# Queue order of weight splits, four-head norms and constants in the root, in a 256-token two-block kernel

## Time and profile before

| what | value |
|---|---|
| median of 3 runs | 3174.78 us (3172.57 to 3176.36) |
| the profiled execution | 3182.96 us, its span 3181.1 us |
| TensorE busy | 2980.7 us (94%) |
| VectorE busy | 1983.2 us (62%) |
| ScalarE busy | 1421.4 us (45%) |
| GpSimd busy | 214.3 us (7%) |
| mean granted TensorE clock | 0.965 of full speed |

### The profile page before, as it was taken

The page is one execution under the profiler, slowest core; times in us unless marked ns, Lnnn a source line. Parts: engine busy times, 40 slices in busy tenths (PEclk is TensorE's granted clock), DMA queues, the critical chain, the costliest instruction groups (busy, mean ns, idle before and its releaser), DMA issues.

```text
span 3181.1 us, 55567 instructions
## 1 busy us (share of the span) xinstructions
PE 2980.7 (94%) x23544; PEld 2902.4 (91%) x23544; DVE 1983.2 (62%) x2232; ACT 1421.4 (45%) x1804; POOL 214.3 (7%) x172
## 2 busy tenths in 40 slices
PE   7998889999999999999997999988799999999986
PEld 7988879999999999999997999976699999999986
DVE  5466776655667666666767676755556555555665
ACT  4345544444444444444445444443444444444443
POOL 1010001100000000000001020111100000000010
PEclk9999899999999999999999999987899999999998
DMA  6634443345555665565554633310266556556553
GB/s 195 182 118 133 121 133 112 122 123 167 176 181 174 186 183 175 174 188 173 182 182 129 190 101 120 107 54 1 70 188 185 179 179 192 182 178 191 174 159 107
DMA packets 251817, 482.24 MB, mean 152 GB/s; under 512 B 16784, under 2 KB 22032, under 8 KB 251440
## 3 DMA queue, kind: packets, MB, share of 16 engines
q1 hardware_dynamic: 251568, 478.68, 49.4%
HBM read 476.53 MB, written 2.10 MB: 150 GB/s over the span
## 4 chain that ended last, share of the span: by engine, by line
PE 58%; DVE 21%; ACT 10%; DMA 5%; issue 4%; POOL 1%; DVEq 0%; POOLq 0%; ACTq 0%
PE psm L393 52%; DVE slo L315 8%; PE psb L447 6%; ACT ar L472 4%; ACT shi L313 4%; DVE ar L475 3%; DVE ar L483 3%; DMA raw<-in_w_up 1%; DMA raw<-in_w_down 1%; DMA raw<-in_w_out 1%; DVE x L475 1%; DVE ar L486 1%; DMA raw<-in_w_ple_gate 1%; DVE hf L486 1%; ACT gh L472 1%
## 5 line engine op out<-in xcount | busy, mean ns | idle before, releaser
L315 DVE TENSOR_TENSOR slo<-raw,shi 128x1024 fp32r<-128x1024 f32 (+1 forms) x901 | 1139.7, 1276 | 788.2 <-ACT shi L313 782.5
L313 ACT ACTIVATE shi<-raw 128x1024 fp32r<-128x1024 f32 (+1 forms) x901 | 930.5, 1050 | 942.9 <-PE psm L393 465.6
L393 PE MATMUL psm<-gh,shi 128*128 128x256 f32 x3664 | 1066.5, 291 | 92.5 <-DVE slo L315 75.1
L393 PE MATMUL psm<-gl,shi 128*128 128x256 f32 x3664 | 1047.4, 286 | 0.0
L393 PE MATMUL psm<-gh,slo 128*128 128x256 f32 x3664 | 1047.0, 286 | 0.0
L393 PE MATMUL psm<-hh,shi 128*128 128x256 f32 x3408 | 980.9, 288 | 39.1 <-DVE slo L315 23.8
L393 PE MATMUL psm<-hl,shi 128*128 128x256 f32 x3408 | 972.5, 285 | 0.0
L393 PE MATMUL psm<-hh,slo 128*128 128x256 f32 x3408 | 972.1, 285 | 0.0
L393 PEld LDWEIGHTS psm<-gh,shi 128*128 128x128 f32 x3664 | 712.9, 195 | 105.3 <-DVE slo L315 81.9
L393 PEld LDWEIGHTS psm<-gl,shi 128*128 128x128 f32 x3664 | 713.1, 195 | 3.4 <-issue 2.7
L393 PEld LDWEIGHTS psm<-gh,slo 128*128 128x128 f32 x3664 | 712.4, 194 | 0.3
(11 more groups left out here) (187 smaller groups left out, 1323.0 us busy)
## 6 DMA issues: line engine op xcount, KB each, us to landing
raw<-in_w_in SPq DMA_DIRECT2D x240, 512.0 KB, 3.7
raw<-in_w_up SPq DMA_DIRECT2D x176, 512.0 KB, 4.1
raw<-in_w_ffn_up SPq DMA_DIRECT2D x128, 512.0 KB, 3.9
raw<-in_w_ffn_down SPq DMA_DIRECT2D x128, 512.0 KB, 4.0
raw<-in_w_down SPq DMA_DIRECT2D x88, 512.0 KB, 4.5
raw<-in_w_out SPq DMA_DIRECT2D x64, 512.0 KB, 4.3
raw<-in_w_ple_gate SPq DMA_DIRECT2D x32, 512.0 KB, 4.9
raw<-in_w_branch_b SPq DMA_DIRECT2D x16, 512.0 KB, 4.6
```

The source lines that it names most:

```text
L313: th = A.do(lambda e: e.activation(shi[:, s, 0:m], raw[:, q, 0:m], ACT.Copy), landed, pe_tok.get(j - NS), chain=False, cost=0.22 + 0.82e-3 ...
L315: lo_tok[j] = V.do(lambda e: e.tensor_tensor(slo[:, s, 0:m], raw[:, q, 0:m], shi[:, s, 0:m].bitcast(F), ALU.subtract), landed, th, chain=F ...
L393: e.matmul(out, l, r, start=st, stop=sp, skip_group_check=True),
```

## The change

In the order of one pass for tile j, both parts of a split now stand at the end of the pass: hi of tile j+4 ahead of the epilogue, lo of tile j+4 (with its fetch of tile j+7) behind the epilogue and ahead of the `fgs` step and the background steps. Four tiles instead of three are split before the first pass. `qk_norm` is replaced by `heads_norm(g)`, in lane 2, queued as soon as the convolution of group g (four heads of q or k) is through: the column sums of four heads go with a 32-column matrix of ones to the four 32-partition quarters of one bank, one root and one reciprocal of 128x256 serve all four, and a matmul from 32 rows with `hsel` spreads each head's row over the partitions again. The end of `gdn` does the same for two heads. The roots read PSUM with scale and bias and the separate multiply-adds go.

```diff
+        def split_hi(j):
+            ...
+            hi_tok[j] = A.do(lambda e: e.activation(shi[:, s, 0:m], raw[:, q, 0:m], ACT.Copy),
+                             landed, pe_tok.get(j - NS), chain=False, cost=0.22 + 0.82e-3 * m)
+        def split_lo(j):
+            ...
             lo_tok[j] = V.do(lambda e: e.tensor_tensor(slo[:, s, 0:m], raw[:, q, 0:m],
                                                        shi[:, s, 0:m].bitcast(F), ALU.subtract),
-                             landed, th, chain=False, cost=0.16 + 1.04e-3 * m)
+                             landed, hi_tok[j], chain=False, cost=0.16 + 1.04e-3 * m)
             if j + NR < len(tiles):
                 issue(j + NR)
@@ group
-                if j + NS - 1 < len(tiles):
-                    split(j + NS - 1)
...
                 cur[1] += 1
+                split_hi(j + NS)
                 if ti == len(ts) - 1:
                     slot.free = epi(slot.ap, pe_tok[j])
+                split_lo(j + NS)
                 for _ in range(fg):
                     fg_step()
                 bg_ready()
@@ Norm.finish
-                tv = ts(rb, b.ap[:, 0:256], 1.0 / D, 1e-6, ALU.mult, ALU.add, tp)
-                ta = act(rb, rb, ACT.Sqrt, tv)
+                ta = act(rb, b.ap[:, 0:256], ACT.Sqrt, tp, scale=1.0 / D, bias=C("eps", 0, 1))
...
-                    stt(r2, b.ap[:, 256:512], 1.0 / D, r2, ALU.mult, ALU.mult)
-                    tv = ts(r2, r2, 1e-6, None, ALU.add, None)
-                    ta = act(r2, r2, ACT.Sqrt, tv)
+                    tv = stt(r2, b.ap[:, 256:512], 1.0 / D, r2, ALU.mult, ALU.mult)
+                    ta = act(r2, r2, ACT.Sqrt, tv, bias=C("eps", 0, 1))
@@ before the first group
-            if f < NS - 1:
-                split(f)
+            split_hi(f)
+            split_lo(f)
@@ end of rope
-                bgs[w] += [moba(w), qk_norm(w)]
+                bgs[w].append(moba(w))
@@ in place of qk_norm
+        def heads_norm(g):
+            buf = (gq, gk)[g // 2][:, 4 * (g % 2):4 * (g % 2) + 4, :]
+            sq, rr = hh_f[:, 0:1024].rearrange("p (a b) -> p a b", a=4), hh_f[:, 1024:1280]
+            yield (g_tok[g],)
+            ta = act(sq, buf, ACT.Square, g_tok[g])
+            yield (ta,)
+            b = bank()
+            tp = mms([(b.ap[32 * f:32 * f + 32, 0:256], C("osel"), sq[:, f, :], True, True) for f in range(4)],
+                     ta, *b.free)
+            ta = act(rr, b.ap[:, 0:256], ACT.Sqrt, tp, bias=C("eps", 0, 1))
+            b.free = (ta,)
+            yield (ta,)
+            tv = rec(rr, ta)
+            yield (tv,)
+            for f in range(4):
+                row = slice(32 * f, 32 * f + 32)
+                b = bank()
+                tp = mms([(b.ap[:, 0:256], C("hsel")[row, :], rr[row, :], True, True)], tv, *b.free)
+                tn = stt(buf[:, f, :], buf[:, f, :], 128 ** -0.5 if g < 2 else 1.0, b.ap[:, 0:256],
+                         ALU.mult, ALU.mult, tp)
+                b.free = (tn,)
+                if f % 2:
+                    yield ()
+            A.wait(tn)
+            qn_tok[g] = tn
@@ epi_gdn
                 g_tok[g] = stt(dst, cth, 1.0, dst, ALU.add, ALU.mult, ta)
+                if g < 4:
+                    bgs[2].append(heads_norm(g))
@@ gdn, end of a pair of heads
-                tp = mms([(b.ap, C("ones"), sq, True, True)], ta, *b.free)
-                te = tp
-                tv = ts(sq, b.ap, 1.0 / 128, 1e-6, ALU.mult, ALU.add, tp)
-                ta = act(sq, sq, ACT.Sqrt, tv)
-                rec(sq, ta)
-                tt(o2, o2, sq.rearrange("p (a b) -> p a b", a=2), ALU.mult)
+                tp = mms([(b.ap[32 * i:32 * i + 32, 0:256], C("osel"), sq[:, 256 * i:256 * i + 256], True, True)
+                          for i in range(2)], ta, *b.free)
+                rr = sq[0:64, 0:256]
+                ta = act(rr, b.ap[0:64, 0:256], ACT.Sqrt, tp, scale=1.0 / 128, bias=C("eps", 0, 1)[0:64, :])
+                tv = rec(rr, ta)
+                for i in range(2):
+                    b = bank()
+                    te = mms([(b.ap[:, 0:256], C("hsel")[32 * i:32 * i + 32, :], sq[32 * i:32 * i + 32, 0:256],
+                               True, True)], tv, *b.free)
+                    b.free = (tt(o2[:, i, :], o2[:, i, :], b.ap[:, 0:256], ALU.mult, te),)
```

More of the change, by code:

```diff
@@ L305, in build @@
         lo_tok, pe_tok = {}, {}
-        def split(j):
+        hi_tok = {}
+        def split_hi(j):
+            if j >= len(tiles):
+                return
             w, r, kc, c, n = tiles[j]
@@ L312, in split @@
             landed = (s_raw[q], 16 * (j // NR + 1))
-            th = A.do(lambda e: e.activation(shi[:, s, 0:m], raw[:, q, 0:m], ACT.Copy),
-                      landed, pe_tok.get(j - NS), chain=False, cost=0.22 + 0.82e-3 * m)
+            hi_tok[j] = A.do(lambda e: e.activation(shi[:, s, 0:m], raw[:, q, 0:m], ACT.Copy),
+                             landed, pe_tok.get(j - NS), chain=False, cost=0.22 + 0.82e-3 * m)
+        def split_lo(j):
+            if j >= len(tiles):
+                return
+            w, r, kc, c, n = tiles[j]
+            m = kc * n
+            s, q = j % NS, j % NR
+            landed = (s_raw[q], 16 * (j // NR + 1))
             lo_tok[j] = V.do(lambda e: e.tensor_tensor(slo[:, s, 0:m], raw[:, q, 0:m],
                                                        shi[:, s, 0:m].bitcast(F), ALU.subtract),
-                             landed, th, chain=False, cost=0.16 + 1.04e-3 * m)
+                             landed, hi_tok[j], chain=False, cost=0.16 + 1.04e-3 * m)
             if j + NR < len(tiles):
@@ L1049, in gdn @@
             sq = inv.Y
-            while len(yb_tok) < 8 or 5 not in g_tok or len(qn_tok) < 2 or "kdec" not in dk:
+            while len(yb_tok) < 8 or 5 not in g_tok or len(qn_tok) < 4 or "kdec" not in dk:
                 yield
             t_g, t_beta, t_kdec = dk["g"], dk["beta"], dk["kdec"]
-            yield (g_tok[5], *yb_tok[-2:], qn_tok[w])
+            yield (g_tok[5], *yb_tok[-2:], qn_tok[3])
             for q in (PE, A, V, P):
-                q.wait(g_tok[5], *yb_tok[-2:], qn_tok[w])
-            tn = qn_tok[w]
+                q.wait(g_tok[5], *yb_tok[-2:], qn_tok[3])
+            tn = qn_tok[3]
             G0, G1 = C("utri", 0, 128), C("utri", 128, 128)
@@ L1157, in gdn @@
                 b = bank()
-                tp = mms([(b.ap, C("ones"), sq, True, True)], ta, *b.free)
-                te = tp
-                tv = ts(sq, b.ap, 1.0 / 128, 1e-6, ALU.mult, ALU.add, tp)
-                b.free = (tv,)
-                ta = act(sq, sq, ACT.Sqrt, tv)
-                yield (ta, *z_tok)
-                rec(sq, ta)
+                tp = mms([(b.ap[32 * i:32 * i + 32, 0:256], C("osel"), sq[:, 256 * i:256 * i + 256], True, True)
+                          for i in range(2)], ta, *b.free)
+                rr = sq[0:64, 0:256]
+                ta = act(rr, b.ap[0:64, 0:256], ACT.Sqrt, tp, scale=1.0 / 128, bias=C("eps", 0, 1)[0:64, :])
+                b.free = (ta,)
+                yield (ta,)
+                tv = rec(rr, ta)
                 while len(z_tok) < 2:
                     yield
-                tt(o2, o2, sq.rearrange("p (a b) -> p a b", a=2), ALU.mult)
+                yield (tv, *z_tok)
+                for i in range(2):
[3 more added lines that the diff above has]
+                    b.free = (tt(o2[:, i, :], o2[:, i, :], b.ap[:, 0:256], ALU.mult, te),)
                 tv = tt(o2, o2, sz[:, hs[0]:hs[0] + 2, :], ALU.mult, *z_tok)
```

## The result

The changed kernel takes 3122.82 us (median of 4 runs, 3120.61 to 3124.47) against 3173.82 us: a ratio of 0.9838, 95% interval 0.9821 to 0.9855. That is 51 us faster; 3126 was forecast. When both were measured again, with the last group of experiments, the medians were 3178.32 and 3120.64, 57.7 us apart; the ratio there, 0.9819 (0.9806 to 0.9833), overlaps the first.

A forecast was written before the change was run, and what follows sets the result against it. TensorE, busy 94% of the span, was taken as the bound, idling mostly in waits for VectorE. Terms -43 + 16 - 18 - 8 + 5 - 0.5 = -48.5 us took 3174.78 to 3126; range 3085 to 3165.

The forecast's parts named there:

- The signs: Listed signs of being right: fewer slo waits, no 512-column reciprocals, additions 6 to 8 us apart, stretch without foreground no longer.
- Bound and clock: From 2300 to 3015 us TensorE never idles, so no gain there; elsewhere waits also bring it back at half clock.
- 170 to 500 us and the price of the matmuls, -43 and +16: Attention, convolutions, q/k norms: 43 us recovered by order and norms together; all new small norm matmuls cost TensorE 16 us more.
- lower bound of 3.6: Extra TensorE time in us if the row-wise small matmuls overlap as the column-wise ones do, 0.90 for each batch.
- Two-head norms at nothing: End of gdn: VectorE saves 8 us, priced at nothing because TensorE is busy 193.8 of 200 us there.
- Stage ends, -18: Where a stage ends and next activations are made: lo fills VectorE's 2.20 us waits; 18 us gained, between 5 and 30.
- My sentence that the late hi delayed the fetch: At stage ends, hi stood behind ScalarE's copies and squares, came late, and so delayed the fetch, since lo frees raw.
- The other groups, -8: From 895 to 1650 us, hi goes ahead of the convolutions; 8 us gained, between 0 and 12.
- Second recurrence, +5: Until 2255 us: background steps at a tile's end wait behind splits; 5 us lost, between 0 and 23.
- Root, -0.5: Last norm at the kernel's end loses 0.42 us and a hop on VectorE; 0.5 us gained.

The follow-up runs named there:

- norms, heads_norm only: Kernel before with only the norms changed, splits in old order: 3148.86 us; kernel before with only heads_norm in place of qk_norm: 3151.06 us.
- the two hybrids: Changed kernel with the old split order where background work is dense: 3109.69 us; the same with each spreading matmul done twice: 3115.88 us.

## Why the prediction was right, step by step

**The signs.** Of those that the prediction named, these came: waits for `slo` between 170 and 500 us fell from 42.7 to 9.8, the reciprocals of 512 columns are gone, the additions at a stage end come 6.71 us apart, and the second feed-forward net takes the same time. Two did not come as written. The granted clock at the stage ends is 0.96, 0.92 and 1.00 (1605 to 1695, 2215 to 2270, 2960 to 3005), so it is above 0.95 at two of three. And the stretch without foreground is 10.2 us longer.

**Bound and clock.** Right: the second feed-forward net takes 645.0 us against 644.2, and nothing was won in it.

**170 to 500 us and the price of the matmuls, -43 and +16.** The sum was right (-27; the stage became 24.9 shorter), both terms were too large. The small matmuls cost 5.4 us more, near the lower bound of 3.6, so what was recovered is about 30. Nearly all of the gain is idle time of TensorE, which fell from 58.3 us (579.50 - 521.23) to 33.8. The step that was off is "I take +16, since the row shown is this shape": the row has single matmuls, 0.62 us apart, while a norm's four can stand together and then cost 0.85 us with the change of shape both ways, where I had counted 4 x 0.62 + 0.4 = 2.9. And I placed the recovery too early: at the mark nearest 450 us (452.4 against 454.2) only 1.8 us were won. Nearly all came in the last 32 tiles of the stage, since background work that is done sooner leaves a stretch of pure weight matmuls there. Their fetches, before and changed:

```profile
634.02 113.34 SPq L300 DMA_DIRECT2D raw<-in_w_in  x32
```

```profile
632.42 89.65 SPq L300 DMA_DIRECT2D raw<-in_w_in  x32
```

I also expected order and norms both to matter there. The runs show that either does part and that the norms suffice. That the cheaper norm is the cause is shown from both sides: the old place with the new cost keeps the gain, the new place with the old cost loses 17 us. Whether it acts by VectorE's load or by the hold on ScalarE is not separated.

**Two-head norms at nothing.** Right within what can be told: the marks show 3 us gained.

**Stage ends, -18.** 3.2 + 10.3 + 4.2 = 17.7 us, with the second end counted from the return of the foreground. The mechanism was right, lo in the 2.20 us gap; the run with hi alone shows that without an early lo nothing is won there. My sentence that the late hi delayed the fetch named the wrong one of the two: with hi early and lo late nothing was gained at the ends, as the lo split is what frees `raw`. The first end (1630 to 1678) gave least.

**The other groups, -8.** The worst term: 16.0 us up to the last `down` tiles and 10.5 in the gated side input, 26.5 in all, more than twice the bound of 12. I read the possible gain from idle time, 9.8 us in 895 to 1650. Here is that stage in the changed kernel (windows, all engines):

```profile
895.00:1589.00 694.00, 694.00 (x5779) 693.79 (x5779) 476.54 (x488) 326.28 (x349) 27.34 (x11) 1.00 0.59 183
```

That is 0.1201 us a matmul. The kernel before needed 755 for 6175, at this rate 741.6, so 13.4 us could be had. A matmul's record lasts about 0.28 us while the next starts after 0.12, and each gap shows some 0.16 short. For the gated side input I had no row after 3060 and let the term lie within the rest.

**Second recurrence, +5.** It cost 8.5 us, between the 0 and 23 that I had given. From the mark near 1678 to the return of the foreground the old order took 576.9 and 576.3 (the kernel before, twice), 576.3 and 572.3 (norms, heads_norm only), 573.0 and 573.4 (the two hybrids). Every kernel with the new order, or with hi alone early, took more: 579.5 to 585.7. The stretch without foreground separates them without doubt: 112.4 to 113.2 us in these six profiles of the old order, 121.3 to 123.5 in the eight others, whatever else differed. With hi early and lo late it is 121.3, so the early hi split alone is enough to make this stretch longer, where I had blamed both splits; moving background steps ahead of lo did not shorten it (122.9). Which step of the recurrence falls behind there stays open.

**Root, -0.5.** 0.9 us in the last group and norm together, within what profiles differ by.

**Luck.** By the profiled executions the terms came to -60.6 where I had -48.5: the other groups gave 18.5 more than I had, the first stage 2 and the recurrence 3.5 less. That the first medians moved by 51, and not by 57.7 as in the second measurement, brought the forecast within 3 us. And +16 with -43 in one sum hid that both were too large.

## What to carry to other kernels

In a statically queued pipeline, look for the instruction that frees a buffer that others wait for (here the lo split, which lets the next fetch start), and put it into the gaps in which its engine waits for another, ahead of work that nobody awaits; here, moving only the instruction that it depends on bought nothing in total. Where a long chain of background work sets the time, the old order was better: look at the stretch in which nothing else runs. Shortening the largest indivisible pieces of the engine that feeds the bound one paid 28 us for 35 us of its time, though on average it was only 62% busy. Price a small matmul by how it stands in the list, single or in a batch. Read what can be won in a stage from its count of matmuls times their pace in an undisturbed stage, not from idle time alone.

## What was not expected of the hardware

24 more small matmuls of 32 rows added 0.26 us each to TensorE's busy time and nothing measurable to the kernel's time; in one batch they held the next weight load back by 0.11 us each, where single ones in a list stood 0.61 to 0.62 us apart.

While one of GpSimd's additions ran (from 2239.83, 3.36 us), one lo split took 1.22 us (2239.70) and the next 2.11 (2242.16). In the old order two took 4.55 together where two others, before GpSimd's addition, took 2.36.
